# Moving weight rounding and silu behind maxima and exponents, and the inverses to the start of a pair, in the attention loops of a two-block kernel

## The reference

```python
# block 2, first layer: every head over context and tokens
sc = einsum(q, k_all) * dh ** -0.5
o  = einsum(softmax(sc), v_all)
y_a = o * silu(ag)                       # and a convolution branch y_b * silu(hg)

# block 2, second layer: windowed heads (with a sink), then neighbourhood heads
p = softmax(concatenate([s_loc + mask, s_ctx, s_sink]))     # windowed
p = softmax(concatenate([s_loc + bias, s_ctx]))             # neighbourhood
y = concatenate([y_w * silu(wg), y_n * silu(ng)])
x = x + gate * (y @ w_out)
```

## Time and profile before

| what | us |
|---|---|
| median of 3 runs | 1581.77 (1581.0 to 1582.0) |
| the profiled execution's own time | 1581.21 |
| span of the profiled execution | 1579.4 |
| PE busy | 1495.0 (95%) |
| DVE busy | 976.8 (62%) |
| ACT busy | 776.2 (49%) |
| first attention, about | 1054 to 1195 |
| second attention, about | 1442 to 1550 |

### The profile page before, as it was taken

One profiled execution on the slowest core, in us unless ns is written; L12 is line 12 of the kernel. 1 busy time (PEld: TensorE's weight loads), 2 busy tenths in 40 slices (PEclk: granted clock), 3 DMA queues, 4 the chain that ended last, 5 costly groups with the idle time before them and its releaser, 6 DMA issues.

```text
span 1579.4 us, 21510 instructions
## 1 busy us (share of the span) xinstructions
PE 1495.0 (95%) x8288; PEld 1201.9 (76%) x8288; DVE 976.8 (62%) x1785; ACT 776.2 (49%) x1301; POOL 64.9 (4%) x132
## 2 busy tenths in 40 slices
PE   6999999999999999998999999989999999989777
PEld 5887777799887787877789987867774367877666
DVE  4554556766544554455766665685589864688675
ACT  4545785455444445787355553335543112444552
POOL 5050000000000000000000000000000000120000
PEclk9999999999999999999999999999999999999999
DMA  8782334697555754333778555442131001543000
GB/s 251 247 192 83 125 116 162 212 249 205 195 182 181 272 183 134 93 122 118 224 219 228 201 175 171 140 114 81 55 83 65 0 5 49 143 132 107 28 28 27
DMA packets 183124, 220.95 MB, mean 140 GB/s; under 512 B 6555, under 2 KB 103365, under 8 KB 183024
## 3 DMA queue, kind: packets, MB, share of 16 engines
q1 hardware_dynamic: 179840, 211.65, 43.0%
q0 software_dynamic: 3184, 7.93, 2.6%
HBM read 216.55 MB, written 3.01 MB: 139 GB/s over the span
## 4 chain that ended last, share of the span: by engine, by line
PE 75%; DVE 14%; ACT 6%; issue 3%; DMA 2%; SPq 0%; DVEq 0%; ACTq 0%
PE bank L598 20%; PE bank L600 20%; PE bank L599 20%; DVE w_low L1721 2%; ACT w_high L1312 2%; PE bank L1065 2%; PE bank L830 1%; PE bank L774 1%; PE bank L1028 1%; PE bank L679 1%; PE bank L805 1%; PE bank L1041 1%; DMA raw<-in_w_up 1%; DVE arena L2175 1%; PE bank L615 1%
## 5 line engine op out<-in xcount | busy, mean ns | idle before, releaser
L1721 DVE TENSOR_TENSOR w_low<-raw,w_high 128x1024 fp32r<-128x1024 f32 x352 | 424.6, 1213 | 383.0 <-ACT w_high L1312 377.7
L1312 ACT ACTIVATE w_high<-raw 128x1024 fp32r<-128x1024 f32 x352 | 366.4, 1046 | 350.6 <-PE bank L600 290.1
L598 PE MATMUL bank<-w_high,acts_r 128*128 128x512 f32 (+1 forms) x848 | 339.8, 401 | 17.6 <-DVE acts_r L1738 6.3
L600 PE MATMUL bank<-w_high,acts_r 128*128 128x512 f32 (+1 forms) x848 | 330.4, 390 | 0.0
L599 PE MATMUL bank<-w_low,acts_r 128*128 128x512 f32 (+1 forms) x848 | 330.3, 390 | 0.0
L598 PE MATMUL bank<-acts_r,w_high 128*128 128x256 f32 (+1 forms) x736 | 230.1, 313 | 9.3 <-DVE arena L2121 5.6
L599 PE MATMUL bank<-acts_r,w_high 128*128 128x256 f32 (+1 forms) x736 | 226.6, 308 | 0.0
L600 PE MATMUL bank<-acts_r,w_low 128*128 128x256 f32 (+1 forms) x736 | 226.6, 308 | 0.0
L598 PEld LDWEIGHTS bank<-w_high,acts_r 128*128 128x128 f32 x848 | 160.8, 190 | 59.9 <-DVE w_low L1721 12.7
L600 PEld LDWEIGHTS bank<-w_high,acts_r 128*128 128x128 f32 x848 | 159.7, 188 | 36.6
L599 PEld LDWEIGHTS bank<-w_low,acts_r 128*128 128x128 f32 x848 | 160.4, 189 | 32.2
(11 more groups left out here) (308 smaller groups left out, 1745.8 us busy)
## 6 DMA issues: line engine op xcount, KB each, us to landing
raw<-in_w_in SPq DMA_DIRECT2D x70, 1024.0 KB, 5.3
raw<-in_w_up SPq DMA_DIRECT2D x64, 512.0 KB, 6.8
raw<-in_w_down SPq DMA_DIRECT2D x32, 1024.0 KB, 5.0
raw<-in_w_ada SPq DMA_DIRECT2D x24, 1024.0 KB, 6.8
raw<-in_w_in SPq DMA_DIRECT2D x32, 512.0 KB, 4.8
raw<-in_w_o SPq DMA_DIRECT2D x8, 1024.0 KB, 7.1
raw<-in_w_out SPq DMA_DIRECT2D x8, 1024.0 KB, 5.0
raw<-in_w_out_c SPq DMA_DIRECT2D x4, 768.0 KB, 5.4
```

What stands on the lines that cost most here:

```text
L598: mm(o, lh, rh, start=start, stop=False)
L600: return mm(o, ll, rh, start=False, stop=stop)
L1312: run(A_(high, src, ACT.Copy), (high_ready, n + 1))
L1721: run(V.tensor_tensor(low, src, high.bitcast(F32), ALU.subtract), (split_ready, n + 1))
```

## The change

In both attentions of block 2:

- DVE begins pair i with the inverses of pair i-1, both units in one instruction over two columns (`invert_sums`), with one signal for the pair (`pair_inverted`), on which PE waits.
- The low parts of late heads come next, ahead of the maxima.
- The maxima follow with no rounding ahead of them, then `take_values(i-2)`, and only then the roundings that are due, and then the silu.
- ACT copies the transposes without a rounding ahead of them, does the exponents, then the rounding that is due, then late heads, and then the exponent for the silu.

```diff
@@ PE, values
                     for side in range(2):
                         pe.wait_ge(*emptied("p", 2 + l, u + side, 0))
-                        pe.wait_ge(*sum_inverted.at(2 + l, u + side))
+                    pe.wait_ge(*pair_inverted.at(2 + l, i))
@@ ACT, attention2
                         n = (2 if U[u][0] == "G" and U[u][2] >= TILES else 4) * P
-                        copy_out(PT2[:, u % 2, 0:n], bank("p", 2 + l, u, 0)[:, 0:n], "p", 2 + l, u, 0)
+                        act.wait_ge(*filled("p", 2 + l, u, 0))
+                        run(A_(PT2[:, u % 2, 0:n], bank("p", 2 + l, u, 0)[:, 0:n], ACT.Copy), emptied("p", 2 + l, u, 0))
                     for u in (2 * i, 2 * i + 1) if i < PAIRS else ():
-                        splits.due("s", 2 + l, u)
...
-                    for key in ended_in[(2 + l, i)]:
-                        take_features(l, key)
+                    if i < PAIRS:
+                        splits.due("s", 2 + l, 2 * i + 1)
                     if l == 1 and i in late_heads:
                         for group in late_heads[i]:
                             take_head_high(*group, due=False)
+                    for key in ended_in[(2 + l, i)]:
+                        take_features(l, key)
@@ DVE, attention2
-                def invert_sum(u):
-                    st = stat[:, u % 4, :, :]
-                    dve.wait_ge(*probs_at(2 + l, u))
-                    if U[u][0] == "W":
-                        run(V.tensor_tensor(st[:, 2, 0:1], st[:, 2, 0:1], st[:, 3, 1:2], ALU.add))
+                def invert_sums(i):
+
+                    sums = stat[:, 2 * i % 4:2 * i % 4 + 2, 2, 0:1]
+                    sinks = stat[:, 2 * i % 4:2 * i % 4 + 2, 3, 1:2]
+                    for u in (2 * i, 2 * i + 1):
+                        dve.wait_ge(*probs_at(2 + l, u))
+                    if U[2 * i][0] == "W":
+                        run(V.tensor_tensor(sums, sums, sinks, ALU.add))
                         run.settle()
-                    run(V.reciprocal(st[:, 2, 1:2], st[:, 2, 0:1]), sum_inverted.by(2 + l, u))
+                    run(V.reciprocal(stat[:, 2 * i % 4:2 * i % 4 + 2, 2, 1:2], sums), pair_inverted.by(2 + l, i))
...
                 for i in range(PAIRS + 2):
+                    if 1 <= i <= PAIRS:
+                        invert_sums(i - 1)
+                    if l == 1 and i - 1 in late_heads:
+                        for group in late_heads[i - 1]:
+                            take_head_low(*group)
                     if i < PAIRS:
-                        splits.due("s", 2 + l, 2 * i)
                         maximum(2 * i)
                         maximum(2 * i + 1)
-                    if 1 <= i <= PAIRS:
-                        invert_sum(2 * i - 2)
-                        invert_sum(2 * i - 1)
                     if i >= 2:
                         take_values(i - 2)
+                    if i < PAIRS:
+                        splits.due("s", 2 + l, 2 * i + 1)
                     if i:
                         for key in ended_in[(2 + l, i - 1)]:
                             take_features(l, key)
-                    if l == 1 and i - 1 in late_heads:
-                        for group in late_heads[i - 1]:
-                            take_head_low(*group)
```

More of the change, by code:

```diff
@@ L451, in two_blocks @@
         bias_ready = Signal(sem("bias_ready"), softs)
-        sum_inverted = Signal(sem("sum_inverted"), softs)
+        sum_inverted = Signal(sem("sum_inverted"), [k for k in softs if k in b1u])
+        pair_inverted = Signal(sem("pair_inverted"), [(l, i) for l in (2, 3) for i in range(len(units_of_block2(l - 2)) // 2)])
         sum_spread = Signal(sem("sum_spread"), [(l, i) for l in (2, 3) for i in range(len(units_of_block2(l - 2)) // 2)])
```

## The result

The changed kernel takes **1600.34 us** (median of four executions, 1599.63 to 1602.42), beside 1581.53 for the kernel before in the same session. The ratio is 1.0118, with a 95% interval of 1.0107 to 1.013: 1.2% slower, 18.8 us. I had said 1595.4, in 1587 to 1603. The profiled execution took 1600.88 us, with a span of 1599.1, which is 19.7 more than before.

What follows compares the result with a forecast made beforehand. PE, busy 95% of the span, was taken to bound the kernel. 5.2 + 2.0 - 1.3 - 0.5 + 5.6 + 2.6 = +13.6 on 1581.2 gave 1594.8, with 0.6 for the median 1595.4 us; range 1587 to 1603.

Steps and rivals of the forecast that it cites:

- The loop: Second attention: PE's values, scores, DVE's maxima and `take_values`; a pair with rounding and silu takes 7.96 us, an unloaded one 4.90.
- M: Second attention: the end of a pair's maxima on DVE, from which the prediction counted the later starts.
- N, +5.2: Second-attention pairs whose inverses have no addition: two take 12.86 us against 11.55, 1.31 slower, four times.
- W, +2.0: Second-attention pairs whose inverses have an addition each: two take 13.01 us against 12.33, 0.68 slower, three times.
- Tail, -0.5: End of the second attention: the rounding ahead of ACT's last copies goes, saving half of its 1.05 us.
- Head, -1.3: Start of the second attention: first maxima gain 1.9 us, but roundings then precede late heads and next maxima; -1.3 taken.
- First attention, +2.6: First attention, silus of 512 columns: DVE's waits for exponent and rounding become 9.6 us against 6.2; +2.6 us in all.
- the rival in which DVE's lateness stops PE there: First attention: DVE's 9.3 us a pair replaces PE's 8.1, six times, +7; with all clock falls 1604 us; chance 0.09.
- The clock, +5.6: Second attention: longer PE waits bring six new clock falls of 1.2 us, one old fall of 1.6 avoided.
- My upper bound of +11: Second attention: upper bound of the cost of PE's clock falls, seven whole ones, in us.
- The forecast's part without the clock: Whole kernel: sum of the other terms, +8.0 us; as a rival with no more clock falls, 1590 us, chance 0.20.
- the rival estimate from the page: DVE, merged reciprocals: a fixed cost of some 150 cycles an instruction would make the sum 2 to 3 us lower.

Runs made afterwards that it cites:

- the kernel with six dummies: Changed kernel plus 6 needless PE matmuls in each of five pairs of the second attention, before values that waited for `take_values`: 1590.68 us, ratio 1.0056.
- the first experiment: New order only in the first attention; the second keeps the order of the kernel before, with merged inverses behind the maxima: 1581.39 us, ratio 0.9996.
- the kernel with 14 dummies: Changed kernel plus 14 needless PE matmuls in each of five pairs of the second attention: 1600.27 us median, one execution 1680.83; ratio without that one 1.0116.

## Why the prediction was right, and where it was off

**The loop.** In the gap shown above `take_values` lets PE start at M + 0.35 (said: 0.34), `w_low` starts at M + 1.84 (1.85) and the next maxima at M + 5.50 (5.57). The ordinary loaded interval is 7.79 (7.96), the one behind it at full clock 4.90 to 4.91 (4.90). That the wait, `w_low` and silu are one block in PE's road is confirmed from the other side by the silu-first and the ACT-early kernels (6.06) and by the later rounding (4.93).

**N, +5.2, and W, +2.0.** The two have to be taken together, because in the kernel before the interval on the border of W and N is a loaded one (6.90) and in the new order it is not (4.90). In the kernel with six dummies the fourteen intervals ahead of the last are 101.0, against 94.5 before: +6.5. The 94.5 have an old fall of the clock in them, at 1457.80, which I had counted with the clock; by the inverses-only kernel it is some 1.3 (7.00 less 5.22, less the 0.5 of the inverses; an estimate). So the order by itself costs about +7.8, where I had said 7.2. The falls around the long wait for the silu are in both kernels and are not separated. The gating and `o3` intervals, counted at nothing beyond the block, are 9.05 - 7.79 = 1.3 above an ordinary one, where before they were 6.25 - 5.03 = 1.2 above an unloaded one. **Tail, -0.5:** 3.75 to 3.12, -0.6.

**Head, -1.3:** 8.39 to 7.63, -0.8. The first maxima moved ahead by 1.7 (1.1 after the first scores, against 2.8). But behind them now stand both roundings, then the inverses and the low part of the late heads, and the first values waited for that:

```profile
1449.99 1.23 DVE L1724 TENSOR_TENSOR w_low<-raw,w_high 128x1024 fp32r<-128x1024 f32 x1 [0.88 <-ACT w_high L1313]
...
1452.25 1.09 PE L1066 MATMUL bank<-arena 128*64 128x128 f32 x16 [0.87 <-DVE hidden_r L2152]
```

**First attention, +2.6.** Measured +2.3 at the last silu of 512 columns, and +1.9 in the first experiment. In the kernels in which `w_low` no longer waits in front of a silu (silu first, ACT early, a pair later) the same stretch takes 143.1 to 143.4, as before. DVE's waits in the stretch of the earlier trace rows answer to the 9.6 that I had worked out:

```profile
DVE w_low L1724 <- ACT w_high L1313: 9.5, 6, 2.2
```

PE stayed full, as in the earlier trace rows, so the rival in which DVE's lateness stops PE there did not come:

```profile
1170.00:1180.00 10.00, 10.00 (x82) 7.87 (x80) 8.45 (x13) 4.64 (x10) 0.00 (x0) 1.00 0.28 105
```

**The clock, +5.6: this term was mis-sized.** It was made of 7.2 for six new falls, less 1.6 for the old one. Six new falls that cost time came (one more, in the second W interval, cost nothing: 8.71 with it, and 8.71 at a granted clock of 1.00 in the kernel with 14 dummies). But the step "I take six new falls of 1.2" took each at less than it cost. Between the changed kernel and the one with six dummies the second attention differs by 121.9 - 111.8 = 10.1, and the stretch behind it by 2.1: 12.2 in the profiled executions, 9.7 in the medians. Behind the five long waits the intervals cost 2.2, 1.2, 2.3, 1.4 and 1.9 over full clock (7.06, 6.11, 7.21, 6.31 against 4.9; 5.03 against 3.12), and the last of these falls runs on into the output product, which is the 2.1. The sixth is in the first W interval (7.68 against 6.73), ahead of every dummy and behind waits of 0.87 and 1.02 only. It is not tied to the long waits: the kernels with 14 and with 6 dummies have the same instructions as the changed one up to there, and one has this fall (7.64) and the other has not.

```profile
1454.58 1.46 PE L1029 MATMUL bank<-acts_r,hidden_r 64*128 64x512 f32 x6 [1.02 <-DVE stat L2179]
...
1456.00:1458.00 2.00, 2.00 (x11) 2.00 (x11) 1.90 (x11) 0.91 (x4) 0.00 (x0) 0.50 0.03 8
```

With the old fall of 1.3 taken off, the term is 10.9 by the profiled executions. My upper bound of +11 was nearer than the value I took. The longest wait I had to go by, apart from the 5.6 for the silu, was 2.3 us; the new ones are 3.15 to 4.60, and all five were followed by a fall, which at 1500.60 to 1506.00 lasts through most of the pair behind. "TensorE: Matmul & The Clock Gate" of the Trainium skill, in the part on the clock gate, has the penalty of the ramp below 1% of a typical kernel's span. The 12.2 are 0.8% of the 1599 us here, but they are only the falls by which these two kernels differ; what all the falls in the kernel cost, no run shows, so this case neither bears the figure out nor speaks against it. Small as the share is, it is over half of what the change cost.

The sum with the terms as measured: 2.3 (up to the second attention), 7.8 (W and N), -0.8 (head), -0.6 (tail) and 10.9 (clock) make 19.6 of the 19.7 of the spans. The forecast's part without the clock was +8.0, and 8.7 is what it stands against. So the mechanism and its size were right, and the time is 5 us above the forecast because of the clock alone. That it still lies in the range is due to the seven whole falls in the upper end.

**Merging the reciprocals.** The prediction went by the overlap of neighbours against a fixed cost an instruction. The row at 1558.74 bears that out: the reciprocal of two columns takes 0.16, and the maxima start 0.07 behind its start. As the rival estimate from the page would have it, the sum should have come out 2 to 3 us lower; without the clock it came out 0.7 above mine. In the inverses-only kernel, work taken out of the road (0.13 a pair, and 0.39 more for W) would be 0.13 x 15 + 0.39 x 7 = 4.7. Its second attention is 4.6 shorter, but about 1.3 of that is the fall that did not come, so the count is somewhat too high.

**What stays open.** How the cost of a single fall comes about (1.2 to 2.3 us in its interval, by when it begins and how long it lasts), why some waits are followed by one and others not, the single executions of 5568 and of 1681 us, and how the W term divides between inverses, late heads and roundings.

## What to carry to other kernels

When deferred work is moved into the idle gap of an engine, list all that ends up in the same gap and compare the sum, with the wait in front of it, to the gap: here 1.6 + 1.15 + 2.5 against 2.3 us. A step that waits for another engine belongs behind the work that doesn't, or in the next gap: the same parts in another order were 25 us faster, and one gap later 34. And where PE begins to wait longer than it did anywhere in the old trace, price a fall of the clock for each such wait (here 1.2 to 2.3 us each, and 4.0 for the last, which ran on into the next stage), not for some of them.

## What the runs showed that I had not expected

- Useless work made the changed kernel faster: 30 dummies of 0.44 us took it from 1600.3 to 1590.7 us. PE's waits for `take_values` went from 20.1 to 7.9 us, none over 1.8, and the granted clock stayed at 1.00 behind them, where it had fallen.
- A float32 matmul of 128x256 against the identity is two instructions and takes 0.44 us (6.21 us for 14).
- Eight waits of DVE for `w_high`, 15.2 us in all, on an engine that is busy 61% of the span, were worth more than their own length: taking five of the eight away and shortening the rest (2.9 us in 3 waits are left in the silu-first kernel) gave back 25 us, with the clock. The kernel before has 18.8 us of such waits at another place in DVE's list, and is faster than the changed one.
